# All 31 taps of a depthwise convolution in one run on VectorE beside the gate product

## What is computed

```python
glu_a, glu_b = jnp.split(c_glu, 2, axis=-1)
u = glu_a * jax.nn.sigmoid(glu_b)                     # the gate product
u = causal_depthwise_conv(u, cnv_dw_w) + cnv_dw_b     # 31 taps, 256 channels
o_b = jax.nn.silu(layer_norm(u, cnv_ln_g, cnv_ln_b))
...
lower = jnp.where(strict, jnp.einsum('nbhcd,nbhsd->nbhcs', kb, kc) * decay, 0.0)
t_inv = lax.linalg.triangular_solve(lower + eye, eye, ...)   # 64x64 inverses
u = jnp.einsum('nbhcs,nbhsd->nbhcd', t_inv, vc * bc)
w = jnp.einsum('nbhcs,nbhsd->nbhcd', t_inv, kb * jnp.exp(gc)[..., None])
```

## Time and profile before

| | |
|---|---|
| median of 3 runs | 3286.78 us (3275.08 to 3292.17) |
| the profiled execution | 3287.24 us, of which the span of the trace is 3285.5 us |
| busy in it | PE 2914.0 us (89%), DVE 1565.6 us (48%), ACT 1038.4 us (32%) |
| mean granted clock of PE | 0.948 |

### The profile page before, as it was taken

One profiled execution on the slowest core, in us unless ns is written; L12 is line 12 of the kernel. 1 busy time (PEld: TensorE's weight loads), 2 busy tenths in 40 slices (PEclk: granted clock), 3 DMA queues, 4 the chain that ended last, 5 costly groups with the idle time before them and its releaser, 6 DMA issues.

```text
span 3285.5 us, 67914 instructions
## 1 busy us (share of the span) xinstructions
PE 2914.0 (89%) x26308; PEld 1893.0 (58%) x26308; DVE 1565.6 (48%) x5142; ACT 1038.4 (32%) x2741; POOL 0.2 (0%) x4
## 2 busy tenths in 40 slices
PE   8879999877888888888888878988999998899998
PEld 7758888764555545555555443454444443456887
DVE  5641016645676767676766723782222200264331
ACT  2120003123555455555454521261111100134220
POOL 0000000000000000000000000000000000000000
PEclk9979999978999999999999988999999999899999
DMA  5113433124999999999999845101122214511331
GB/s 208 66 64 129 153 141 103 40 69 141 322 325 325 325 317 322 322 319 316 322 321 317 302 159 223 64 1 51 64 77 77 77 64 195 215 65 52 141 143 75
DMA packets 205858, 576.06 MB, mean 175 GB/s; under 512 B 6496, under 2 KB 6624, under 8 KB 179040
## 3 DMA queue, kind: packets, MB, share of 16 engines
q1 hardware_dynamic: 205536, 571.72, 50.5%
HBM read 570.65 MB, written 1.05 MB: 174 GB/s over the span
## 4 chain that ended last, share of the span: by engine, by line
PE 58%; DMA 23%; DVE 13%; issue 2%; ACT 2%; DVEq 1%; SPq 1%; ACTq 0%
PE P L475 43%; DMA ring<-ws_moe 20%; PE P L843 5%; DVE arena L1776 4%; DMA ring<-ws_b 2%; DVE ring L1776 2%; PE P L558 1%; PE P L913 1%; DVE small L1443 1%; PE P L568 1%; DVEq L1773 1%; DVE X_sb L1519 1%; PE P L577 1%; PE P L526 1%; PE P L811 1%
## 5 line engine op out<-in xcount | busy, mean ns | idle before, releaser
L475 PE MATMUL P<-arena,ring 128*128 128x256 f32 (+1 forms) x2784 | 903.7, 486 | 16.8 <-ACT arena L1098 16.7
L475 PEld LDWEIGHTS P<-arena,ring 128*128 128x128 f32 x2784 | 533.6, 192 | 375.5 <-issue 327.3
L843 PE MATMUL P<-arena 128*32 128x256 f32 x6496 | 369.4, 380 | 12.7 <-DVE Y L1754 5.1
L843 PE MATMUL P<-ring,arena 128*32 128x256 f32 x4256 | 281.7, 416 | 86.0 <-DMA ring<-ws_moe 76.6
L475 PE MATMUL P<-X_sb,ring 128*128 128x256 f32 x1504 | 337.5, 385 | 3.9 <-ACT X_sb L1079 3.9
L475 PEld LDWEIGHTS P<-X_sb,ring 128*128 128x128 f32 x1504 | 287.5, 193 | 46.1 <-issue 6.2
L1776 DVE COPY arena<-ring 128x256 f32 x1120 | 234.7, 289 | 155.1 <-DMA ring<-ws_moe 139.6
L843 PEld LDWEIGHTS P<-arena 128*32 128x32 f32 x6496 | 213.9, 110 | 151.3 <-DVE ring L1776 11.1
L1776 DVE COPY arena<-arena 128x256 f32 x1120 | 233.8, 289 | 70.3 <-DMA arena<-ws_moe 56.3
L843 PEld LDWEIGHTS P<-ring,arena 128*32 128x32 f32 x4256 | 148.6, 120 | 204.6 <-DMA ring<-ws_moe 89.1
L1282 ACT ACTIVATE arena<-ring 128x256 f32 x560 | 181.3, 404 | 230.3 <-DMA ring<-ws_moe 168.6
(11 more groups left out here) (361 smaller groups left out, 2611.6 us busy)
## 6 DMA issues: line engine op xcount, KB each, us to landing
ring<-ws_moe SPq DMA_DIRECT2D x84, 2048.0 KB, 13.2
arena<-ws_moe SPq DMA_DIRECT2D x84, 2048.0 KB, 13.7
ring<-ws_b SPq DMA_DIRECT2D x137, 1024.0 KB, 4.8
ring<-ws_a SPq DMA_DIRECT2D x67, 1024.0 KB, 4.9
cst_sb<-cst SPq DMA_DIRECT2D x1, 1664.0 KB, 8.6
X_sb<-xT SPq DMA_DIRECT2D x1, 1024.0 KB, 4.9
X_sb<-ctxT SPq DMA_DIRECT2D x1, 1024.0 KB, 4.8
out<-Y SPq DMA_DIRECT2D x2, 512.0 KB, 2.6
```

What stands on the lines that cost most here:

```text
L475: ins = nc.tensor.matmul(bank(i, n), blockap(s, b % SLOT), rhs(kk), start=kk == 0, stop=kk == k - 1)
L843: ins = nc.tensor.matmul(acc(g // 2)[BR * j:BR * (j + 1), g % 2], x[:, b * BR:(b + 1) * BR], weights_of(b), start=k == 0, stop=last and kk ...
```

## The change

The taps' calls inside and before the levels are gone, and the first call makes all of them:

```diff
@@ -1570,7 +1570,7 @@
                     L(v.tensor_scalar(cacc[:, m, :], upad[:, m, 0:T], pv[:, w:w + 1], v_(f"dwb{l}", m), ALU.mult, ALU.add))
-                taps(1, 3)
+                taps(1, CONVK)
                 for h in range(2):
                     V.take("gram")
@@ -1580,11 +1580,9 @@
                 L(v.tensor_tensor(kg, kn, gb(el, HD), ALU.mult))
-                taps(3, 11)
                 for h in range(2):
                     V.take("gram")
                     L(v.tensor_tensor(half(AT, h), P1h(1, h), half(decT, h), ALU.mult), "gram_read")
-                taps(11, 17)
                 for lev in range(1, 6):
@@ -1594,8 +1592,6 @@
                         L(v.tensor_tensor(g3(MT[lev % 2]), g3(LT), mb(clevel(lev + 2)), ALU.mult), "level_in")
-                    if lev < 5:
-                        taps(14 + 3 * lev, 17 + 3 * lev if lev < 4 else CONVK)
```

## The result

| | |
|---|---|
| before | 3284.61 us, median of 6 runs |
| changed | 3303.0 us, median of 6 runs |
| ratio | 1.0062, 95% interval 1.0037 to 1.0086, that is +12 to +28 us |
| the profiled executions | 3287.24 us before, 3297.97 us changed |

The change makes the kernel slower by 0.6%. The forecast was 3304 us, in a range from 3295 to 3317 us. The ratio is an estimate over all runs and not the quotient of the two medians, which is 1.0056 (+18.4 us); so the interval lies a little above that.

The account below looks back on a forecast made before the run. PE was taken to bound the kernel on average, DVE in the levels. Per layer 19.1 us added at the gate less 10.7 us saved gave +8.4, twice +16.8 us on 3287.24 us: 3304 us, range 3295 to 3317 us.

Parts of the forecast that it names:

- The gate: Sixty tap instructions after the gate product delay start_in; PE stands still 17.3 us, the next tile comes 18.9 us late.
- The clock after the gate: After PE's restart at line 640 the clock returns in 3.1 us; tile 17 loses 0.2 us, added total 18.6 to 20.
- The levels: Without taps each of the inverse's levels takes about 4.45 us; 10.7 us a layer saved, half clock before U included.
- The half clock behind the gap of 3.38 us: Before the chunks for U the gap goes, so their pair costs 1.55 instead of 2.82 us, 1.3 us saved.
- The sum: Per mixer layer, 19.1 us added less 10.7 us saved, +8.4 us; over two layers +16.8 us.
- B: Rival: hand-overs hold each level without taps at some 5.5 us; net +25 us, 3312 us; chance 0.08.
- C: Rival: after the gate stall PE stays at half rate until level 1; +55 us, 3342 us; chance 0.04.
- D: Rival: PE runs tiles 17 to 21 during the wait for start_in; about 3268 us; chance 0.03.

Follow-up runs that it names:

- e1: Kernel before with taps 17 to 29, which stood in the levels, left out of the computation; 3258.97 us, ratio 0.9923.
- e2: Kernel before with taps 1 to 16 in one run (32 instructions) after the gate product, levels as before; 3298.73 us, ratio 1.0047.
- e7: Kernel before with taps 1 to 14 (28 instructions) after the gate product, levels as before; 3286.69 us, ratio 1.0018.
- e8: Changed kernel with tiles 17 to 20 moved ahead of line 640's two chunks in PE's stream; 3278.06 us, ratio 1.0000.
- e3: Kernel before with taps 11 to 30 all placed before level 1, none in the levels; 3273.3 us, ratio 0.9977.
- e5: Changed kernel with DVE's identity additions, which raise start_in, placed after the other instructions of both halves; 3303.37 us, ratio 1.0072.
- e4: Kernel before with all taps kept but laid where the traces show DVE with room; 3259.99 us, ratio 0.9931.
- e6: Changed kernel with taps 26 to 29 (8 instructions) left out of the computation; 3291.55 us, ratio 1.0045.

## Why the prediction was right, point by point

**The gate.** A wait of 17.3 us was forecast, 17.26 us was measured, in both layers; tile 17 was to be 18.9 us late and is 111.26 - 91.99 - 0.23 = 19.0 us late (91.99 us is its start in the timeline before; 0.23 us is what this run had lost before the gate). The taps cost 0.521 us each in the long run too (31.25 us from the first of the 60 to line 1576). This step was right to 0.1 us.

**The clock after the gate** is the term that was mis-sized. I took 0.2 us for tile 17, from one instance of a return after 3.1 us, with 0.9 us as the upper bound. Measured: tile 17 took 5.22 us in layer 0 and 5.06 us in layer 1 instead of 3.72 us, 1.5 and 1.3 us. So what is added came to 20.5 and 20.4 us a layer, beyond the term's upper bound of 20 us, and two of the signs named did not come: the clock was at 1.00 by 114.3 us and not by 113 us, and level 1 started at 131.8 us and not at about 130 us. The bound was too narrow because it was built from a single row; the time of such a return varies between 2.7 and 9.5 us in this study.

**The levels.** 4.45 us a level was forecast, 4.44 us measured; 10.7 us to be saved up to line 721, and measured (145.08 - 111.02) - (155.06 - 131.79) = 10.8 us in layer 0, where 145.08 us is the start of line 721 before. In layer 1 it is 9.7 us, because of the two breaks of 0.65 and 0.38 us. The half clock behind the gap of 3.38 us went away with the gap, as forecast.

**The sum.** Forecast +8.4 us a layer. Measured by the same marks: 20.5 - 10.8 = +9.8 us in layer 0 and 20.4 - 9.7 = +10.7 us in layer 1, +20.5 us together instead of +16.8. The difference of 3.7 us is the clock at tile 17 (1.3 and 1.1 us over the 0.2 us put in), 0.1 us a layer in the tile's start, and the breaks of layer 1 (1.0 us). The median came out at +18.4 us and the interval is +12 to +28 us, so +17 and +20.5 are both in it. That 3304 us lies within 1 us of 3303.0 us is luck: the forecast was added to an execution of 3287.24 us, and the median before came to 3284.61 us over six runs, and a single execution varies by more than this in the stage of the experts.

**The rivals.** B is excluded by e1 and the changed kernel's rows. C in its full form did not happen (tiles 18 to 21 ran at the full clock), but a part of it did, 1.5 and 1.3 us in the two layers, and in e2 2.8 and 2.5 us. The prediction also read from the kernel before that waits of 1.67 us leave the clock at 1.00. That held in most of the rows here, but in e7's layer 1 it fell beside them and fell again soon after its return. D did not happen, and e8 shows that it would have taken a change of PE's stream: with it the gate's price falls from 20.5 to about 7.8 us a layer (118.75 against 111.02 us in layer 0), below the 10.8 us of the gain, though the total of e8 can't be told from before.

**Chances.** I put 0.58 on slower by over 0.5% and 0.39 on the same, since +17 us lay on the edge. The measured +0.62% is just over it, with an interval that reaches under it.

## What to carry to other kernels

Filler work (here the taps, which no other engine waits for soon) on an in-order engine is free only where that engine has room before its next consumer comes; reckon the room at each place (here 4.95 us of waiting plus 6 us of earliness at the gate, 8.6 us before level 1, 0.8 us in a level) and fill it up to that, instead of gathering the work in one place. Both ends of such a move can be read from one trace: the wait it makes from the start of the filler, and what it gives back from an instance of the loop without filler, as level 1 was here. Price a new wait of TensorE with some half clock on top: every wait of 2.67 us and more at line 640 in these ten profiles had it, and it cost 2.8 and 2.5 us in e2 and 1.8 us in e3. Don't take a single restart as its size.

## What the runs showed of the hardware that I had not expected

- The granted clock of TensorE fell in e2 although no wait reached the 3.38 us of the kernel before: in layer 1 it fell 0.15 us after a wait of 2.68 us had ended. Waits of 0.59 and 0.86 us in e7 left it at 1.00. The cost in e2 was 2.8 and 2.5 us a layer.
- Waits of 1.67 and 0.17 us in each level left the clock at 1.00 in both layers of the kernel before and of e2, and in layer 0 of e7, but not in layer 1 of e7, where it fell in level 5.
- From PE's restart to the full clock 2.7 to 9.5 us passed; neither the length of the stall nor a break of 0.23 us orders these times.
- In layer 1 PE stopped early in level 2 with nothing that the trace shows as a cause: for 0.65 us in the changed kernel, in e2 and in e5, for 0.92 us in e8 and for 0.33 us in e7, each time after the first 159 records of the levels. It did not in the kernel before, in e1, e3, e4 or e6, and never in layer 0. It is left open.
